# A two-block transformer kernel on one core: the first row's scale and shift moved to ScalarE, the start reordered, memory stores moved

## The chip, the cores and the metric

The kernel runs on one core of a Trainium2 chip (trn2). The metric is device time in microseconds (us), from one launch to its end; the number compared is the median of several runs. TensorE (PE), VectorE (DVE), ScalarE (ACT), GpSimd (POOL) and SyncE (SP) are the core's five engines. They run their own instruction streams in order and meet at semaphores. SP and POOL issue the DMAs here.

## What is computed

Two transformer blocks on 256 tokens of 1024 features, in float32. The first block is conditioned by a vector c: six slices of `silu(c) @ ada_w + ada_b` give a shift, a scale and a gate for each half of the block.

```python
mod = silu(c) @ ada_w + ada_b
shift1, scale1, gate1, shift2, scale2, gate2 = split(mod, 6)
u = rms_norm(h, norm1_g) * (1 + scale1) + shift1
z = u @ w_in                      # q, k, v of two attentions, gates
mixed = (sigmoid(m_a) * y_a + sigmoid(m_b) * y_b) @ w_out
h = h + gate1 * mixed
h = h + gate2 * (relu(rms_norm(h, norm2_g) * (1 + scale2) + shift2) @ w1)**2 @ w2
# second block: x + swiglu/2, then spatial gating + latent attention
# + attention over a memory of 256 rows (rms_norm(mem) @ w_kv), then x + swiglu/2
x = x + merged @ w_out_2
x = x + 0.5 * swiglu(rms_norm(x, ffn2_norm), w_gu, w_down)
```

## The kernel before

**Layout and stream.** Activations are kept feature-major: 8 blocks `k` of 128 features by 256 tokens. The weights arrive as one stream of slots of 8 tiles (128x1024 float32, 512 KB) in a ring of six. To keep float32 accuracy every operand is split in a rounded high part and a low part: ACT rounds a slot (L1413, `round_slot`), DVE subtracts (L1873, `split_slot`), and TensorE does three products per tile (hi·hi, hi·lo, lo·hi; `project`), or two with a 512 wide one (`project_wide`, hi times both parts side by side). Of the activations `u` and `u_lo` are the two parts. On ACT and DVE the call `ahead(name, reach)` puts the splitting of all slots up to the one that `name` uses, plus a reach, at this place of the engine's stream; `output`, `taken` do the same and wait for a PSUM bank to be full or freed.

**The first stage.** c (one row) goes through Tanh on ACT (L1488) and a multiply on DVE (L1948), TensorE spreads it over the partitions (`spread_c`), DVE copies it to `c_row` (L1953). Meanwhile ACT squares x, TensorE sums the squares (`x_ss`) and ACT makes `row_rinv` (L1454, L1456). Each of the 16 first columns of `mod` is one reduction of a 512 KB tile with `c_row` on DVE (`ada_sum`, L1929, an instruction and a short read of its accumulator): for each block k first the scale column, then the shift column. TensorE then runs one stage per block k, 48 matmuls of two slots (2k and 2k+1), once block k of `u` and `u_lo` is there. On DVE stage k reads: split of slot 2k, low part of u (L1975), split of slot 2k+1, the two `ada_sum` of block k+1, the scale column times the gain (L1967), and x times scale times `row_rinv` (L1969). On ACT: round slot 2k, add the shift and round (L1498), round slot 2k+1. TensorE fills the time at the start with matmuls on ones (`keep_warm`, 8 ahead of `spread_c`, 6 behind the small product `bias`, which needs the two small tables `buckets` and `table`).

**Further places.** POOL's stream holds the other 32 tiles of `ada` in a ring of three (L1316), the load of `bias` (L1334), the two stores of the memory's normalised parts (L1338, L1340), and their loads back. The stick-breaking attention works in `sbw`, 12 blocks of `wide`, at blocks 16 to 27, and starts once both memory stores have landed. In the last product of the second block's mix, `add_and_split` (L2182 adds the product to x, L2261 makes the low part of u) hands over to `project_first_two`, which takes two banks at once (f2g0, f2u0): the second is the bank of mix2_6. The last product `f2d7` is a `project_wide`, so two additions follow it (L2253, L2254) before the last store.

## Time and profile before

| | us |
|---|---|
| median of 3 runs | 1038.56 (1038.42 to 1039.31) |
| the profiled run | 1034.66 |
| its span, first to last instruction | 1032.9 |

The profile is of one run; its span lies 1.8 us under that run's own time, and that run lies 3.9 us under the median. Columns of a timeline row: start in us, length in us, engine, line, operation, output<-input, shape, how many in a row; in brackets the idle time of the engine before it and what ended it. A busy TensorE row is a modelled length; the distance between starts tells the pace.

### The profile page before, as it was taken

The numbers are of one execution on the slowest core, as the hardware profiler recorded it, in microseconds if no ns is written. First come the engines' busy times: TensorE is split into PE (matmuls) and PEld (weight loads), VectorE is DVE, ScalarE is ACT, GpSimd is POOL, SyncE is SP. The second block draws the span as 40 slices with busy tenths as digits, with TensorE's granted clock in tenths as the row PEclk, the third lists the DMA queues.
The fourth block names the chain that finished last, engine by engine and source line by source line (L and its number), as shares of the span: only waits on it lengthen the run. The fifth ranks groups of instructions, "written<-read, shape, count | busy, mean of one in ns | idle before, by whom it ended". The sixth has DMA issues, their size and how long they took to land.

```text
span 1032.9 us, 18991 instructions
## 1 busy us (share of the span) xinstructions
PE 1025.3 (99%) x6926; PEld 933.1 (90%) x6926; DVE 808.3 (78%) x1486; ACT 614.8 (60%) x1140; POOL 47.3 (5%) x74
## 2 busy tenths in 40 slices
PE   8999999999999999999999999999999999999998
PEld 7999998999988888888888899899999998888887
DVE  7998988988988555598887867666877869888753
ACT  5497688547665444565654557796554466555532
POOL 1011100020100000000000100000000010000000
PEclk9999999999999999999999999999999999999999
DMA  9998855776866666666666655555445546666663
GB/s 355 411 359 286 275 174 165 234 260 218 307 186 186 191 191 185 183 187 190 191 187 187 190 175 164 154 153 164 123 123 153 174 149 200 189 192 189 185 191 113
DMA packets 58366, 208.94 MB, mean 202 GB/s; under 512 B 7041, under 2 KB 8449, under 8 KB 57771
## 3 DMA queue, kind: packets, MB, share of 16 engines
q1 hardware_dynamic: 52474, 184.72, 58.2%
q0 software_dynamic: 5808, 23.09, 6.4%
q8 instruction: 55, 0.90, 0.4%
q14 instruction: 29, 0.23, 0.1%
HBM read 204.62 MB, written 3.16 MB: 201 GB/s over the span
## 4 chain that ended last, share of the span: by engine, by line
PE 92%; DVE 6%; issue 2%; ACT 1%; DVEq 0%; ACTq 0%
PE bank L682 90%; DVE ring_rounded L1873 2%; PE bank L1043 1%; DVE ada_ring L1929 1%; DVE body L1929 0%; DVE u L1969 0%; DVE u_rounded L1975 0%; ACT body L1573 0%; DVE body L1989 0%; ACT rounded_rounded L1413 0%; DVE body L2163 0%; ACT body L1505 0%; DVE body L2167 0%; DVE part L2163 0%; DVE body L2118 0%
## 5 line engine op out<-in xcount | busy, mean ns | idle before, releaser
L682 PE MATMUL bank<-u_rounded,rounded_rounded 128*128 128x256 f32 (+1 forms) x2152 | 506.8, 328 | 1.4 <-issue 1.0
L1873 DVE TENSOR_TENSOR ring_rounded<-ring,rounded_rounded 128x1024 fp32r<-128x1024 f32 x326 | 397.2, 1224 | 114.1 <-ACT rounded_rounded L1413 103.2
L1413 ACT ACTIVATE rounded_rounded<-ring 128x1024 fp32r<-128x1024 f32 x326 | 342.8, 1054 | 111.5 <-PE bank L682 100.6
L682 PE MATMUL bank<-u_rounded,ring_rounded 128*128 128x256 f32 x1504 | 350.3, 281 | 0.0
L682 PEld LDWEIGHTS bank<-u_rounded,rounded_rounded 128*128 128x128 f32 x2152 | 332.7, 188 | 4.9 <-issue 2.0
L682 PE MATMUL bank<-body_rounded,rounded_rounded 128*128 128x256 f32 (+1 forms) x1296 | 321.1, 335 | 0.2 <-DVE body L2163 0.2
L682 PEld LDWEIGHTS bank<-u_rounded,ring_rounded 128*128 128x128 f32 x1504 | 282.8, 188 | 37.1
L682 PE MATMUL bank<-body_rounded,ring_rounded 128*128 128x256 f32 x952 | 217.0, 280 | 0.0
L682 PEld LDWEIGHTS bank<-body_rounded,ring_rounded 128*128 128x128 f32 x952 | 178.9, 188 | 26.4
L682 PEld LDWEIGHTS bank<-body_rounded,rounded_rounded 128*128 128x128 f32 x1296 | 201.1, 188 | 1.4 <-issue 0.4
L1668 ACT ACTIVATE part<-bank 128x256 f32<-128x256 f32 x65 | 24.9, 383 | 78.5 <-PE bank L682 78.5
L1929 DVE CUSTOM_DVE_ANT_0 ada_ring<-ada_ring,ada_acc,cols 128x1024 f32<-128x1024 f32 x38 | 48.4, 1279 | 0.2 <-DMA ada_ring<-in_ada 0.2
L1361 POOL TENSOR_TENSOR turned<-turned 128x256 f32<-128x256 f32 x20 | 18.3, 914 | 572.3 <-ACT turned L1844 248.1
L2229 DVE TENSOR_TENSOR part<-bank,part 128x256 f32<-128x256 f32 x65 | 27.5, 424 | 17.5 <-ACT part L1668 17.4
L1573 ACT ACTIVATE body<-body,stats 128x128 f32<-128x128 f32 (+2 forms) x64 | 25.9, 407 | 15.4 <-DVE stats L2442 15.4
L1668 ACT ACTIVATE body<-bank 128x256 f32<-128x256 f32 x42 | 16.1, 383 | 31.8 <-PE bank L682 31.8
L1643 ACT ACTIVATE body_rounded<-body 128x256 fp32r<-128x256 f32 x76 | 31.2, 411 | 5.2 <-DVE body L2331 4.1
L2154 DVE TENSOR_TENSOR body_rounded<-body,body_rounded 128x256 fp32r<-128x256 f32 x76 | 31.8, 418 | 1.1 <-ACT body_rounded L1643 1.0
L682 PE MATMUL bank<-rounded_rounded,u_rounded 128*128 128x512 f32 (+1 forms) x96 | 28.1, 364 | 1.5 <-ACT lines L1502 1.5
L2229 DVE TENSOR_TENSOR body<-bank,body 128x256 f32<-128x256 f32 x42 | 17.8, 424 | 14.2 <-ACT body L1668 14.0
L1316 POOL DMA_DIRECT2D ada_ring<-in_ada x32 | 17.2, 537 | 173.7 <-DVE mod L1929 168.8
L682 PEld LDWEIGHTS bank<-rounded_rounded,u_rounded 128*128 128x128 f32 x96 | 17.0, 188 | 4.3 <-issue 1.7
(276 smaller groups left out, 892.2 us busy)
## 6 DMA issues: line engine op xcount, KB each, us to landing
ring<-in_stream SPq DMA_DIRECT2D x328, 512.0 KB, 3.7
ada_ring<-in_ada POOLq DMA_DIRECT2D x32, 512.0 KB, 5.4
body<-in_ada SPq DMA_DIRECT2D x8, 512.0 KB, 9.2
ada_ring<-in_ada SPq DMA_DIRECT2D x6, 512.0 KB, 8.3
mem_parts_kept<-body_rounded POOLq DMA_DIRECT2D x2, 1024.0 KB, 7.3
body_rounded<-mem_parts_kept POOLq DMA_DIRECT2D x2, 1024.0 KB, 5.2
x<-in_x_t SPq DMA_DIRECT2D x2, 512.0 KB, 4.7
body<-in_mem_t SPq DMA_DIRECT2D x2, 512.0 KB, 7.0
```

Of the source, the lines that this page charges most:

```text
L682: return nc.tensor.matmul(out, lhs, rhs, start=start, stop=stop, skip_group_check=True)
L1043: return nc.tensor.transpose(ps[:, at_col:at_col + P], src, mat("ident"))
L1316: pool.dma_start(ada_ring[:, n % ADA_RING, :], ada[ADA_EARLY + n]).then_inc(ada_full[n % ADA_RING], 16)
L1361: ins = pool.tensor_tensor(row_squares[:, i, :], row_squares[:, i - 1, :], row_squares[:, i, :], ALU.add)
L1413: a(R(slot_round(q)), slot_weights(n), ACT.Copy).then_inc(slot_rounded, 1)
L1573: ins = a(dst, src, ACT.Exp, scale=-1.0 if i < 8 else 1.0, bias=stats[:, i % 2, 0, k:k + 1], accum_out=stats[:, i % 2, 1, k:k + 1])
L1643: a(R(hidden[:, i, :]), hidden_lo[:, i, :], ACT.Copy).then_inc(hidden_rounded, 1)
L1668: a(dst, bank(name)[:, T:2 * T], ACT.Copy).then_inc(half_copied, 1)
L1873: v.tensor_tensor(R(w), w, R(slot_round(q)), ALU.subtract).then_inc(slot_split, 1)
L1929: v.tensor_tensor_reduce(out=w, in0=w, in1=c_row, scale=0.5, scalar=col("ada_b", at), op0=ALU.mult, op1=ALU.add, accum_out=mod[:, at:at + ...
L2154: v.tensor_tensor(R(hidden_lo[:, i, :]), hidden_lo[:, i, :], R(hidden[:, i, :]), ALU.subtract).then_inc(hidden_ready, 1)
L2229: free(v.tensor_tensor(dst, bank(name)[:, 0:T], dst, ALU.add), name)
```

## The change

- **c in two halves.** Tanh, multiply and copy of c are done for columns 0 to 511 and 512 to 1023 apart; the copies to `c_row` stand ahead of the wait for `cols`.
- **Slots 0 and 1 ahead of the small tables** in SP's order of loads.
- **Scale and shift on ACT.** DVE only multiplies x by `row_rinv` (`normed_x`), between the scale sum and the shift sum of a block. ACT makes scale times gain plus gain (128x1), then u rounded and u plain with scale and shift in one pass each (two 128x256), then rounds slot 2k+1. DVE's low part is a plain subtraction.
- **Two slots (16, 17) are split before DVE adds the memory's squares.**
- **Memory stores later and in parts**; `bias` is loaded after the first head of the stick-breaking attention is evacuated; `sbw` lies in blocks 12 to 23; `mats` is loaded in two parts, the second and `pos` by POOL.
- **In the second mix** both last additions to x come before low parts 4 to 6.
- **f2d7 is a plain `project`**, followed by one addition.

```diff
-MATRICES = ["ones", "ident", "halves", "q_even", "q_odd", "rotate", "neg_suffix",
-            "neg_ones", "before", "not_before", "not_after", "spread"]
+MATRICES = ["ones", "ident", "halves", "neg_suffix", "neg_ones", "before", "not_before", "spread",
+            "q_even", "q_odd", "rotate", "not_after"]
+LATE_MATRICES = 8
...
-        sbw = flat(wide[:, 16:28, :]).rearrange("p (a b c) -> p a b c", a=2, b=4)
+        sbw = flat(wide[:, 12:24, :]).rearrange("p (a b c) -> p a b c", a=2, b=4)
...
             for k in range(RING // 2):
                 load_ada_early(k)
+                for r in (2 * k, 2 * k + 1):
+                    load(r, r)
                 if k == 0:
                     sp.dma_start(buckets, buckets_d).then_inc(loaded["bias_in"], 16)
                     sp.dma_start(table[:, :], table_d).then_inc(loaded["bias_in"], 16)
-                for r in (2 * k, 2 * k + 1):
-                    load(r, r)
...
             load_ada(0, ADA_RING)
+            load_ada(ADA_RING, ADA_RING + ADA_IN_KEYS)
+            pool.wait_ge(u_rounded, ROW_MEM * KD + KD // 2)
+            pool.dma_start(mem_parts_kept[0, :, 0:4, :], R(mem_n[:, 0:4, :])).then_inc(mem_hi_stored, 16)
+            evacuated(pool, "cmp_hid_k")
+            load_ada(ADA_RING + ADA_IN_KEYS, ADA_RING + ADA_BEFORE_SB)
+            evacuated(pool, "sbz0")
+            pool.wait_ge(u_rounded, (ROW_MEM + 1) * KD)
+            pool.dma_start(mem_parts_kept[0, :, 4:8, :], R(mem_n[:, 4:8, :])).then_inc(mem_hi_end_stored, 16)
             pool.wait_ge(bias_stored, 16)
             pool.dma_start(bias, bass.AP(bias_rows.tensor, bias_rows.offset, [[1, P], [512, 8], [1, T]])
                            ).then_inc(loaded["bias"], 16)
-            load_ada(ADA_RING, ADA_RING + ADA_IN_KEYS)
-            pool.wait_ge(u_rounded, (ROW_MEM + 1) * KD)
-            pool.dma_start(mem_parts_kept[0], R(mem_n)).then_inc(mem_stored, 16)
+            load_ada(ADA_RING + ADA_BEFORE_SB, ADA_RING + ADA_BEFORE_SB + 2)
             pool.wait_ge(u_ready, (ROW_MEM + 1) * KD)
-            pool.dma_start(mem_parts_kept[1], R(mem_n_lo)).then_inc(mem_stored, 16)
+            pool.dma_start(mem_parts_kept[1], R(mem_n_lo)).then_inc(mem_lo_stored, 16)
...
-            a(c_tanh, c_line, ACT.Tanh, scale=0.5).then_inc(c_tanh_ready, 1)
+            for h in c_halves:
+                a(c_tanh[:, h], c_line[:, h], ACT.Tanh, scale=0.5).then_inc(c_tanh_ready, 1)
...
             for k in range(KD):
+                scale, shift, gain = mod[:, KD + k:KD + k + 1], mod[:, k:k + 1], col("norm1_g", k)
+                act.wait_ge(ada_summed, 2 * k + 1)
+                a(scale, scale, ACT.Identity, scale=gain, bias=gain).then_inc(scale_ready, 1)
                 ahead(f"u{k}", 1)
-                act.wait_ge(u_normed, ROW_X * KD + k + 1)
+                act.wait_ge(scale_ready, k + 1)
+                act.wait_ge(x_normed, k + 1)
                 act.wait_ge(ada_summed, 2 * k + 2)
-                a(R(u[:, k, :]), u_lo[:, k, :], ACT.Identity, bias=mod[:, k:k + 1]).then_inc(u_rounded, 1)
+                a(R(u[:, k, :]), u_lo[:, k, :], ACT.Identity, scale=scale, bias=shift).then_inc(u_rounded, 1)
+                a(u_lo[:, k, :], u_lo[:, k, :], ACT.Identity, scale=scale, bias=shift).then_inc(u_normed, 1)
                 ahead(f"u{k}", 2)
...
-            sum_early(0)
-            scaled(0)
+            def sum_early_with_x(k):
+                sum_early(2 * k)
+                if k == 0:
+                    dve.wait_ge(row_rinv_ready, ROW_X + 1)
+                normed_x(k)
+                sum_early(2 * k + 1)
+
+            sum_early_with_x(0)
             for k in range(KD):
                 ahead(f"u{k}", 1)
                 low_part_of_u(k)
                 ahead(f"u{k}", 2)
                 if k < KD - 1:
-                    sum_early(k + 1)
-                    scaled(k + 1)
+                    sum_early_with_x(k + 1)
+            ahead("vsw0", 3)
...
                 add_mixed(5)
                 ahead(f"{last}6")
+                add_mixed(6)
                 low_part(4)
+                add_mixed(7)
+                evacuated(dve, f"{last}{KD - 1}")
                 low_part(5)
-                add_mixed(6)
                 low_part(6)
                 ahead(f"{last}7")
-                add_mixed(7)
-                evacuated(dve, f"{last}{KD - 1}")
                 low_part(KD - 1)
...
-                    add_both(f"{p}d{m}", m, 0.5)
+                    if row == ROW_4 and m == KD - 1:
+                        add_residual(f"{p}d{m}", m, 0.5, reach=False)
+                    else:
+                        add_both(f"{p}d{m}", m, 0.5)
```

How the instructions stand on DVE at the first block and into the second, before (ISA on a 128x1024 tile is `ada_sum`, ISA on 128x1 its accumulator read; `ring_rounded` is the split of a slot):

```order
L1929 ISA ada_ring,mod<-ada_ring,ada_acc,cols 128x1024 [waits ada_early_full1]
L1929 ISA mod 128x1
L1967 SCALAR_TENSOR_TENSOR mod<-mod,cols 128x1 [waits ada_summed]
L1969 SCALAR_TENSOR_TENSOR u<-x,mod,row_rinv 128x256 [waits row_rinv_ready,dve_step]
L1873 TENSOR_TENSOR ring_rounded<-ring,rounded_rounded 128x1024 [waits slot_rounded]
L1975 SCALAR_TENSOR_TENSOR u_rounded<-u,mod,u_rounded 128x256 [waits u_rounded]
L1873 TENSOR_TENSOR ring_rounded<-ring,rounded_rounded 128x1024 [waits slot_rounded]
```

And in the change:

```order
L1950 ISA ada_ring,mod<-ada_ring,ada_acc,cols 128x1024 [waits ada_early_full0]
L1950 ISA mod 128x1
L1986 TENSOR_TENSOR u<-x,row_rinv 128x256 [waits row_rinv_ready]
L1950 ISA ada_ring,mod<-ada_ring,ada_acc,cols 128x1024 [waits ada_early_full1]
L1950 ISA mod 128x1
L1894 TENSOR_TENSOR ring_rounded<-ring,rounded_rounded 128x1024 [waits slot_rounded]
L1992 TENSOR_TENSOR u_rounded<-u,u_rounded 128x256 [waits u_normed,u_rounded]
```

The multiply of x, which waits for `row_rinv`, stood behind both sums of the block and now stands between them.

On ACT, the same stretch before, from the end of `row_rinv` on:

```order
L1456 ACTIVATE row_rinv<-log_ms 128x256 [waits bank_free0]
L1413 ACTIVATE rounded_rounded<-ring 128x1024 [waits slot_full0,row_rinv_ready]
L1498 ACTIVATE u_rounded<-u,mod 128x256 [waits ada_summed,u_normed]
L1413 ACTIVATE rounded_rounded<-ring 128x1024 [waits slot_full1]
L1502 ACTIVATE lines<-bank 8x512 [waits bank_full1]
```

And in the change:

```order
L1470 ACTIVATE row_rinv<-log_ms 128x256 [waits bank_free0]
L1512 ACTIVATE mod<-mod,cols 128x1 [waits ada_summed,row_rinv_ready]
L1427 ACTIVATE rounded_rounded<-ring 128x1024 [waits slot_full0]
L1517 ACTIVATE u_rounded<-u,mod 128x256 [waits ada_summed,x_normed,scale_ready]
L1518 ACTIVATE u<-u,mod 128x256
L1427 ACTIVATE rounded_rounded<-ring 128x1024 [waits slot_full1]
```

Two more instructions stand on ACT for each block, one of them between the rounding of u and that of slot 2k+1.

On DVE in the second mix, from the fifth addition on, before (bank 2 is mix2_6, bank 0 mix2_7):

```order
L2182 SCALAR_TENSOR_TENSOR x<-bank,x 128x256 [waits bank_full6]
L1873 TENSOR_TENSOR ring_rounded<-ring,rounded_rounded 128x1024 [waits slot_rounded]
L2261 SCALAR_TENSOR_TENSOR u_rounded<-x,cols,u_rounded 128x256 [waits u_rounded] x2
L2182 SCALAR_TENSOR_TENSOR x<-bank,x 128x256 [waits bank_full2]
L2261 SCALAR_TENSOR_TENSOR u_rounded<-x,cols,u_rounded 128x256 [waits u_rounded]
```

And in the change:

```order
L2204 SCALAR_TENSOR_TENSOR x<-bank,x 128x256 [waits bank_full6]
L1894 TENSOR_TENSOR ring_rounded<-ring,rounded_rounded 128x1024 [waits slot_rounded]
L2204 SCALAR_TENSOR_TENSOR x<-bank,x 128x256 [waits bank_full2]
L2283 SCALAR_TENSOR_TENSOR u_rounded<-x,cols,u_rounded 128x256 [waits u_rounded]
L2204 SCALAR_TENSOR_TENSOR x<-bank,x 128x256 [waits bank_full0]
L2283 SCALAR_TENSOR_TENSOR u_rounded<-x,cols,u_rounded 128x256 [waits u_rounded,bank_free0]
```

The addition that empties bank 2 moved ahead of two low parts.

## Rows read from the trace of the kernel before

**Rows 1.** Page, part 1: busy time and share of the span by engine.
```profile
PE 1025.3 (99%) x6926; PEld 933.1 (90%) x6926; DVE 808.3 (78%) x1486; ACT 614.8 (60%) x1140; POOL 47.3 (5%) x74
```

**Rows 2.** Timeline of TensorE (PEld its weight loads), from the start on.
```profile
1.14 3.61 PE L682 MATMUL bank<-mats 128*128 128x128 f32 x16 [1.14 <-DVE mats L1946]
...
10.24 0.09 PEld L682 LDWEIGHTS bank<-lines,table 33*8 33x8 f32 x2 [0.33 <-DMA table<-in_table]
...
11.19 1.60 PE L682 MATMUL bank<-mats 128*128 128x128 f32 x12
...
14.34 0.36 PE L682 MATMUL bank<-rounded_rounded,u_rounded 128*128 128x256 f32 x1 [1.55 <-ACT lines L1502]
```

**Rows 3.** Busy time in six stages: engines in us, PEclk, DMA share, GB/s.
```profile
20.20:54.40 34.20, 34.20 (x253) 32.52 (x252) 33.98 (x55) 15.18 (x19) 1.94 (x4) 1.00 1.02 409
```

**Rows 4.** Timeline of DVE, block 0.
```profile
11.46 0.48 DVE L1969 SCALAR_TENSOR_TENSOR u<-x,mod,row_rinv 128x256 f32<-128x256 f32 x1
...
13.60 0.48 DVE L1975 SCALAR_TENSOR_TENSOR u_rounded<-u,mod,u_rounded 128x256 fp32r<-128x256 f32 x1
```

**Rows 5.** Timeline of DVE, from block 1's last sum to block 2's second.
```profile
17.54 0.08 DVE L1929 DVE_READ_ACCUMULATOR2_ANT mod<- 128x1 f32 x1
...
17.73 0.48 DVE L1969 SCALAR_TENSOR_TENSOR u<-x,mod,row_rinv 128x256 f32<-128x256 f32 x1
...
19.26 0.48 DVE L1975 SCALAR_TENSOR_TENSOR u_rounded<-u,mod,u_rounded 128x256 fp32r<-128x256 f32 x1
19.74 1.23 DVE L1873 TENSOR_TENSOR ring_rounded<-ring,rounded_rounded 128x1024 fp32r<-128x1024 f32 x1
20.88 1.28 DVE L1929 CUSTOM_DVE_ANT_0 body<-body,ada_acc,cols 128x1024 f32<-128x1024 f32 x1
...
22.09 1.28 DVE L1929 CUSTOM_DVE_ANT_0 body<-body,ada_acc,cols 128x1024 f32<-128x1024 f32 x1
```

**Rows 6.** Timeline of ACT, end of row_rinv and block 1.
```profile
10.92 0.42 ACT L1456 ACTIVATE row_rinv<-log_ms 128x256 f32<-128x256 f32 x1
...
18.25 0.51 ACT L1498 ACTIVATE u_rounded<-u,mod 128x256 fp32r<-128x256 f32 x1 [0.87 <-DVE u L1969]
18.66 1.04 ACT L1413 ACTIVATE rounded_rounded<-ring 128x1024 fp32r<-128x1024 f32 x1
```

**Rows 7.** Timeline of TensorE, start of stage 7 and of the next product.
```profile
54.42 0.36 PE L682 MATMUL bank<-rounded_rounded,u_rounded 128*128 128x256 f32 x1
...
60.55 0.36 PE L682 MATMUL bank<-u_rounded,rounded_rounded 128*128 128x256 f32 x1 [0.23 <-DVE ring_rounded L1873]
```

**Rows 8.** Timelines of DVE, then TensorE, at the end of the second mix.
```profile
841.72 1.83 DVE L2261 SCALAR_TENSOR_TENSOR u_rounded<-x,cols,u_rounded 128x256 fp32r<-128x256 f32 x2
843.48 0.41 DVE L2182 SCALAR_TENSOR_TENSOR x<-bank,x 128x256 f32<-128x256 f32 x1
...
842.75 0.28 PE L682 MATMUL bank<-body_rounded,ring_rounded 128*128 128x256 f32 x1
843.99 0.36 PE L682 MATMUL bank<-u_rounded,rounded_rounded 128*128 128x256 f32 x1 [0.96 <-issue]
...
847.26 0.28 PE L682 MATMUL bank<-u_rounded,ring_rounded 128*128 128x256 f32 x1
847.57 0.39 PE L682 MATMUL bank<-u_rounded,rounded_rounded 128*128 128x256 f32 x1
```

**Rows 9.** Timeline of DVE at the end of the kernel.
```profile
1029.76 0.42 DVE L2253 SCALAR_TENSOR_TENSOR x<-bank,x 128x256 f32<-128x256 f32 x1 [6.78 <-PE bank L682]
1030.22 0.42 DVE L2254 SCALAR_TENSOR_TENSOR x<-bank,x 128x256 f32<-128x256 f32 x1
```

**Rows 10.** Timelines of DVE, then TensorE, in the stick-breaking attention (heads 3 to 5).
```profile
113.31 1.28 DVE L1929 CUSTOM_DVE_ANT_0 ada_ring<-ada_ring,ada_acc,cols 128x1024 f32<-128x1024 f32 x1 [0.15 <-DMA ada_ring<-in_ada]
...
115.32 0.28 DVE L2034 TENSOR_TENSOR body<-body,mats 128x128 f32<-128x128 f32 x1
...
118.18 1.14 PE L682 MATMUL bank<-body,mats 128*128 128x256 f32 x6
```

73 lines of the change are left out of this document (39 added, 34 removed).

## The prediction

> **What bounds the kernel now.** I read the busy shares first: TensorE 99% of the span [rows 1], nothing else above 90%. The chain of waits agrees: it runs through TensorE from 60.55 on but for a few knots. So only four kinds of time can move: the start until TensorE has its first real matmul (14.34 [rows 2]), the first eight stages if another engine paces them, the few holes later, and what stands behind the last matmul. Everything else, the memory stores among it, has TensorE's work as cover.
>
> In the first stages DVE is busy 33.98 of 34.20 us [rows 3] and repeats every 5.75 us (worked out below). TensorE's stage 0 begins at 14.34, stage 7 at 54.42 [rows 2, 7]: 40.08 for seven, 5.73 each. The six stages of [rows 3] have it busy for 34.20 us without a gap, so it needs 5.70 for one at most. The two are nearly level, and a slower loop on DVE or ACT shows at once.
>
> **Start-up.** Halving c gains almost nothing: the warm-up matmuls hold TensorE until 4.75 [rows 2], where c's product started anyway. I take 0.1 us, so `row_rinv`, done at 11.34 [rows 6], is done at 11.25. Then the order on DVE costs: the second sum now stands behind the multiply that waits for `row_rinv`, where before both sums were done by the time the multiply began (11.46 [rows 4]). The multiply has no row of its own kind; the nearest is the old one, 0.48 long [rows 5], of which some 0.08 overlaps the next; with one factor fewer I take 0.38 (bounds 0.34 and 0.40). Second sum 11.68 to 12.96 (1.28 [rows 5]); call its end t. ACT then makes its two passes and rounds slot 1, DVE splits slot 0 (1.14) and takes the low part (0.42): ready at 14.5 against 14.08. So the first stage could start 0.4 later.
>
> The small tables are a second brake. TensorE began `bias` at 10.24, after 0.33 of waiting for them [rows 2]. Behind slots 0 and 1, 1.05 MB, at 409 GB/s [rows 3] they come 2.6 us later, at 12.8. Bias to first warm-up is 0.95 (10.24 to 11.19), the warm-up 1.60 [rows 2]: stage 0 starts at about 15.3 instead of 14.34. That is 0.9 late, but TensorE can catch up as long as DVE is behind it.
>
> The granted clock is part of this. The 16 warm-up records at 1.14 take 3.61, the 12 at 11.19 take 1.60 [rows 2]: the first are at the 1.2 GHz level, the later at 2.4 GHz, and the 1.55 us of idleness before 14.34 did not lower it. Now the idleness lies ahead of `bias` and is 2.6 us long. The Trainium skill (TensorE: Matmul & The Clock Gate, What's actually happening) says that an idle array falls back to half rate. By that rule bias and warm-up may run at the lower level; the trace, with its shorter hole, doesn't decide it.
>
> **The loop of the eight stages.** Before, from t (17.62 in block 1): scale and multiply, ACT's shift at 18.25, its rounding of slot 2k+1 at 18.66 for 1.04, DVE's split at 19.74, sums at 20.88 and 22.09, the end 1.28 later at 23.37 [rows 5, 6]: 5.75. DVE's split waits for ACT here (19.74 is 0.04 after ACT's end). Now ACT's first pass can begin at t+0.04, the second 0.41 later, the rounding another 0.41 later (18.25 to 18.66), its end at t+1.90, the split at t+1.94 instead of t+2.12. But the multiply, 0.38, now stands between the sums: 1.94 + 1.14 + 1.21 + 0.38 + 1.28 = **5.95**. DVE has less work (it now idles about 0.35 per block behind ACT), yet the loop through both engines is 0.2 longer. The pass that was saved on DVE came back on ACT ahead of the rounding that DVE waits for.
>
> From there: block 1's t is 18.9 (12.96 + 5.95), block 7's 54.6, its low part 1.56 later (1.14 + 0.42) at 56.2, TensorE at most 0.26 behind that (14.34 after 14.08 in block 0); I take 56.3. Its last stage is 5.73 long like the others. End at 62.0. Before, the next product began at 60.55 instead of 60.15 (54.42 + 5.73), since DVE added the memory's squares before it split slot 16 [rows 7]. The change splits slots 16 and 17 first: ACT has slot 15 rounded at 56.5, then eight squares of at most 0.41 each, slot 16 by 60.8 at the latest, DVE splits it by 62.0, just in time. Sum of the first part: 62.0 - 60.55 = **+1.5 us**. The late start (15.3) is swallowed: 15.3 + 2 x 5.70 = 26.7, where DVE allows stage 2 at 26.5 and falls behind from then on.
>
> The Trainium skill (ScalarE: Activation LUTs, Rules for kernel authors) says to put additions and multiplications on VectorE. It speaks against this edit; the trace agrees only in part, since a pass is 0.51 on ACT and 0.48 on DVE [rows 5, 6]: the engine isn't dearer, the place is.
>
> **The second mix.** TensorE ends mix2_7 at 842.75 and starts f2g0 at 843.99, since the pair of banks needs mix2_6 added to x; that addition (843.48 to 843.89) stood behind two low parts of 0.92 each [rows 8]. Now it starts at 841.72 and the banks are free at 842.2, before TensorE arrives. A second, small wait follows: 847.26 to 847.57, for u's last block [rows 8]; its addition moves from behind a split to 843.1, so that goes too. Without both the 28 matmuls between run from about 842.95 and end at 846.35 instead of 847.57 (pace (847.26 - 843.99)/27 = 0.121, with the first a little longer): **-1.2 us**. Next are the low parts of blocks 5 to 7 on DVE, wanted from 846.8 on, ready by 846.6: bound 0 to 0.5 for that, I take 0.
>
> **The end.** One addition fewer: 1030.22 - 1029.76 = 0.46 [rows 9]. The plain product has 66 matmuls of 256 columns for 22 of 512 and 22 of 256: the same columns, 22 starts more. A start costs about 0.01 beyond its columns (0.118 pace against 0.107 for 256 columns at 2.4 GHz), 0.2 in all, less 0.1 for a shorter last one. **-0.3 us** (bounds -0.5 and -0.2).
>
> **Stores, `bias`, matrices, `sbw`.** POOL's queue gets other neighbours. `bias` is loaded some 40 us later, yet 20 us before its first use; ACT and DVE no longer wait for both stores at the first head, a wait that TensorE never felt. Zero, with the cover named in the second rival.
>
> **Sum.** +1.5 - 1.2 - 0.3 = 0.0. The span stays 1032.9, the profiled run 1034.7, and the median, to which I carry the difference, at 1038.5.
>
> **Rivals.**
> 1. *The first stages are not slower.* If ACT's second pass and rounding overlap more, or the multiply hides, TensorE paces: start 15.3, eight times 5.70, end 60.9, +0.4. Against it: ACT starts its instructions 0.41 apart in every row. Sum -1.1: 1037.4. It decides if the loop is under 5.7.
> 2. *The moved store collides, and the kernel is slower.* The 1 MB store of the low parts goes out near 105 us between tiles of `ada`. DVE waited for such a tile at 113.31 already (0.15), softplus of head 5 was done at 115.60, TensorE wanted it at 118.18 [rows 10]: cover 2.6 us. The store alone takes 2.6 us at 409 GB/s and 5 if it gets half. It decides from 2.6 us of delay; at 5 us TensorE loses 2.4. Sum +2.4: 1040.9.
> 3. *The clock drops in the hole before `bias`.* Bias and warm-up at the lower level are 0.95 + 1.6 longer, stage 0 at 17.8, eight stages of 5.70 to 63.4: 1.4 more than forecast, 1039.9. It decides if 2.6 us of idleness are enough where 1.55 were not. [...]
> 4. *The mix doesn't gain.* Should low part 4 (0.92, slowed) or the slot's split be late, half of 1.2 is left: 1039.1.
>
> **How the numbers follow.** Forecast 0.50, its own range 1037.8 to 1039.3 (the multiply 0.34 to 0.40 is 0.3 over seven blocks, the end 0.3, the low parts 0.5). Rival 1: 0.18. Rival 2: 0.14, the upper half of its price in doubt. Rival 3: 0.10. Rival 4: 0.08. A measurement of this kernel tells about 0.2%, 2.1 us, from no change. Only rival 2 at its full price, or two of the upper ones together, is slower by that: 0.13. Faster by that needs rival 1 with gains that I don't see: 0.07. Same: 0.80. The range reaches past rival 1 and most of rival 2: 1036.9 to 1040.7.
>
> **What the profile will show.** DVE's low part of u every 5.95 us with a gap of 0.3 to 0.4 put down to ACT's rounding before each split of an odd slot (right), or no gap and 5.70 (rival 1). `bias` on TensorE at 12.8, stage 0 at about 15.3, the next product at 62.0 with no hole. Warm-up records of 12 in 1.6 us or in 2.6 (rival 3). f2g0 less than 0.3 after mix2_7, and the end of the kernel 0.3 closer to the last matmul. Gaps of DVE before `ada_sum` near 115 would be rival 2. I am wrong if the first stages are paced by TensorE, or if a new hole over 0.5 us stands anywhere between 62 us and the mix.

## The result

The changed kernel is slower: 1043.13 us in the median of 15 runs (1038.68 to 1044.4), against 1038.98 (1034.8 to 1043.84) for the kernel before in 15 runs beside it. The ratio is 1.0035, with a 95% interval of 1.0019 to 1.0050. The profiled run took 1038.79 us with a span of 1037.1; before it was 1034.66 with 1032.9, so the trace shows 4.2 us to explain. The forecast was 1038.5, no change, with a range up to 1040.7. Both the time and the direction were wrong.

One thing must be known to read the times below. The runs of nearly every kernel here lie in two clusters some 4 us apart (before: 1034.7 to 1037.3 and 1038.2 to 1044.5; after: medians of 1038.79 and 1043.41), because TensorE's clock rises either by 5 us from the start of the span or only at 12.7 to 13.9; the section on the hardware shows it. So I compare the medians of the clusters, and traces from the end of this start on. All ratios are over all runs, and this spread makes their intervals wide.

| start of, us | before | after | difference |
|---|---|---|---|
| `row_rinv` on ACT | 10.92 | 11.03 | 0.1 |
| stage 0 on TensorE | 14.34 | 15.84 | 1.5 |
| the product behind the eight stages | 60.55 | 64.01 | 3.5 |
| the matmul on the sum of the memory's squares | 66.33 | 70.39 | 4.1 |
| attention, the product at 133.85 before | 133.85 | 139.37 | 5.5 |
| the part behind the attention, the product at 199.78 before | 199.78 | 205.66 | 5.9 |
| f2g0 behind the second mix | 843.99 | 848.82 | 4.8 |
| f2g0, last block of u | 847.57 | 852.14 | 4.6 |
| last addition to x | 1030.22 | 1034.36 | 4.1 |

Read downwards, the difference grows in three places (stages, squares, attention), a little in a fourth (0.4 by 200), and falls at the mix and at the end.

### The profile page after: what moved, and what is told of

The parts are those of the page before. It is cut to its first block, busy times and chain, and to the rows that moved or that the text cites. A ratio compares the mean times of both kernels' runs of the same rounds, so it can differ in the third digit from the quotient of the medians.

```text
span 1037.1 us, 19048 instructions
## 1 busy us (share of the span) xinstructions
PE 1027.4 (99%) x6948; PEld 935.5 (90%) x6948; DVE 805.5 (78%) x1478; ACT 621.5 (60%) x1157; POOL 49.4 (5%) x77
## 4 chain that ended last, share of the span: by engine, by line
PE 88%; DVE 7%; ACT 2%; issue 1%; DMA 1%; ACTq 0%; DVEq 0%
PE bank L685 87%; DVE ring_rounded L1894 2%; DVE ada_ring L1950 2%; PE bank L1046 1%; DVE body L1950 1%; ACT rounded_rounded L1427 1%; DMA ada_ring<-in_ada 1%; ACT u L1518 0%; ACT body L1593 0%; DVE u L1986 0%; DVE body L2053 0%; ACT body L1525 0%; DVE body L2011 0%; DVE body L2185 0%; DVE part L2185 0%
## 5 line engine op out<-in xcount | busy, mean ns | idle before, releaser
L685 PEld LDWEIGHTS bank<-body_rounded,rounded_rounded 128*128 128x128 f32 x1318 | 204.5, 188 | 1.7 <-DVE body L2185 0.7
```

The lines of the kernel that those rows point to most:

```text
L685: return nc.tensor.matmul(out, lhs, rhs, start=start, stop=stop, skip_group_check=True)
```

## The profile after

**The start and the first stages.** TensorE's timeline, answering to [rows 2]:

```profile
12.77 1.02 PE L685 MATMUL bank<-lines,table 33*8 33x512 f32 x2 [2.35 <-DMA table<-in_table]
13.72 1.87 PE L685 MATMUL bank<-mats 128*128 128x128 f32 x12
15.84 0.55 PE L685 MATMUL bank<-rounded_rounded,u_rounded 128*128 128x256 f32 x1 [0.24 <-issue]
...
22.74 0.28 PE L685 MATMUL bank<-rounded_rounded,u_rounded 128*128 128x256 f32 x1
```

The tables land at 12.8 as forecast. The 12 warm-up matmuls take 1.87 instead of 1.60 and the first matmul of stage 0 0.55 instead of 0.36: the clock went to its lower level behind the 2.35 us hole (granted clock 0.68 from 14.3 to 16 us, 0.71 from 16 to 20). Stage 0 lasts 6.90 (15.84 to 22.74) instead of some 5.8. Stage 0 begins 0.10 behind the end of ACT's copy of the small product (15.74); before, it waited for the same copy (14.25, start at 14.34 [rows 2]):

```profile
15.17 0.57 ACT L1522 ACTIVATE lines<-bank 8x512 f32<-8x512 f32 x1
```

DVE and ACT in block 1, answering to [rows 5] and [rows 6]:

```profile
19.18 1.22 DVE L1894 TENSOR_TENSOR ring_rounded<-ring,rounded_rounded 128x1024 fp32r<-128x1024 f32 x1
20.58 0.43 DVE L1992 TENSOR_TENSOR u_rounded<-u,u_rounded 128x256 fp32r<-128x256 f32 x1 [0.18 <-ACT u L1518]
21.46 1.23 DVE L1894 TENSOR_TENSOR ring_rounded<-ring,rounded_rounded 128x1024 fp32r<-128x1024 f32 x1 [0.45 <-ACT rounded_rounded L1427]
22.60 1.28 DVE L1950 CUSTOM_DVE_ANT_0 body<-body,ada_acc,cols 128x1024 f32<-128x1024 f32 x1
...
23.81 0.42 DVE L1986 TENSOR_TENSOR u<-x,row_rinv 128x256 f32<-128x256 f32 x1
24.14 1.28 DVE L1950 CUSTOM_DVE_ANT_0 body<-body,ada_acc,cols 128x1024 f32<-128x1024 f32 x1
```

```profile
19.38 0.60 ACT L1517 ACTIVATE u_rounded<-u,mod 128x256 fp32r<-128x256 f32 x1 [0.28 <-DVE mod L1950]
19.89 0.59 ACT L1518 ACTIVATE u<-u,mod 128x256 f32<-128x256 f32 x1
20.39 1.04 ACT L1427 ACTIVATE rounded_rounded<-ring 128x1024 fp32r<-128x1024 f32 x1
```

A pass with both operands takes 0.60, and the next starts 0.50 to 0.51 later, where [rows 6] have 0.51 and 0.41. DVE now waits twice in a block, 0.18 for the second pass and 0.45 for the rounding of the odd slot. The low part of block 0 began at 14.42, so a block takes 6.16. TensorE follows DVE from stage 5 on, as its wait before stage 7 shows:

```profile
58.15 0.36 PE L685 MATMUL bank<-rounded_rounded,u_rounded 128*128 128x256 f32 x1 [0.26 <-DVE u_rounded L1992]
...
67.47 0.47 PE L685 MATMUL bank<-u_rounded,rounded_rounded 128*128 128x256 f32 x2 [0.36 <-DVE ring_rounded L1894]
...
70.39 0.38 PE L685 MATMUL bank<-body,mats 128*128 128x256 f32 x1
```

The hole before 67.47 is new. On DVE the sums of the squares now stand where the next slot's split is wanted:

```profile
63.00 2.40 DVE L2011 TENSOR_TENSOR body<-body 128x1024 f32<-128x1024 f32 x3
...
66.11 1.22 DVE L1894 TENSOR_TENSOR ring_rounded<-ring,rounded_rounded 128x1024 fp32r<-128x1024 f32 x1
```

**The attention**, answering to [rows 10]. DVE's waits for tiles of `ada` (sum, number, longest), before and then after:

```profile
DVE ada_ring L1929 <- DMA ada_ring<-in_ada: 0.2, 1, 0.2
```

```profile
DVE ada_ring L1950 <- DMA ada_ring<-in_ada: 4.0, 2, 3.4
```

DMA issues from 104 to 124 (how many, KB, median us to landing), before and then after:

```profile
ada_ring<-in_ada POOLq DMA_DIRECT2D x8, 512.0 KB, 5.5
```

```profile
ada_ring<-in_ada POOLq DMA_DIRECT2D x6, 512.0 KB, 6.8
mem_parts_kept<-body_rounded POOLq DMA_DIRECT2D x1, 1024.0 KB, 9.6
```

The store went out at 108.67, the tile behind it at 112.00, and DVE could read that tile at 120.61. In TensorE's timeline this wait comes back as three holes, which put it 0.7, 0.4 and 0.35 us further behind the kernel before:

```profile
122.96 0.81 PE L685 MATMUL bank<-body,mats 128*128 128x256 f32 x3 [0.65 <-DVE body L2056]
...
128.22 0.70 PE L685 MATMUL bank<-body,mats 128*128 128x256 f32 x2 [0.31 <-DVE body L2056]
...
139.37 0.61 PE L1046 MATMUL bank<-mats,body 128*15 128x128 f32 x4 [0.53 <-DVE body L2140]
```

**The mix and the end**, answering to [rows 8] and [rows 9]. TensorE, then DVE:

```profile
848.70 0.28 PE L685 MATMUL bank<-body_rounded,ring_rounded 128*128 128x256 f32 x1
848.82 0.28 PE L685 MATMUL bank<-u_rounded,rounded_rounded 128*128 128x256 f32 x1
```

```profile
1034.36 0.42 DVE L2204 SCALAR_TENSOR_TENSOR x<-bank,x 128x256 f32<-128x256 f32 x1 [6.95 <-PE bank L685]
```

f2g0 starts 0.12 behind the last matmul of the mix, with no wait, and one addition closes the kernel.

## The experiments

My theory from this trace was a sum: the loop of the stages, which runs through ACT (+3.5 with the start), the squares ahead of a split (+0.5), the store between tiles (+1.5), the mix (-1.5), the end (-0.3). Its rivals were that the late start with its low clock costs the first part, and that the holes in the attention come from something else than the store.

Since the start differs from run to run, I measure the first part from the start of `row_rinv` to the start of the matmul on the squares' sum (10.92 and 66.33 before, 11.03 and 70.39 after):

| kernel | `row_rinv` | squares | first part | against before |
|---|---|---|---|---|
| before | 10.92 | 66.33 | 55.41 | |
| after | 11.03 | 70.39 | 59.36 | +3.95 |
| e1, old order on POOL | 10.71 | 70.07 | 59.36 | +3.95 |
| e2, scale on DVE | 11.15 | 66.59 | 55.44 | 0.0 |
| e3, roundings ahead | 11.11 | 73.42 | 62.31 | +6.9 |
| e4, mix and end alone | 14.89 | 70.30 | 55.41 | 0.0 |
| e5, tables first | 15.30 | 74.66 | 59.36 | +3.95 |
| e6, e3 mended | 15.41 | 73.36 | 57.95 | +2.5 |
| e7, no scale operand | 15.03 | 72.92 | 57.89 | +2.5 |
| e9, combined | 15.12 | 72.01 | 56.89 | +1.5 |
| e10, slots 16, 17 ahead | 15.10 | 70.14 | 55.04 | -0.4 |
| e12, POOL's order alone | 10.95 | 66.37 | 55.42 | 0.0 |
| e13, squares first | 15.09 | 74.58 | 59.49 | +4.1 |
| e14, as e4 | 15.51 | 70.93 | 55.42 | 0.0 |

Kernels without an edit in this part agree to 0.01 us, whatever the start (before, e4, e12, e14), so 0.1 us can be read here.

**e1, the old order on POOL's queue.**

```diff
             load_ada(0, ADA_RING)
-            load_ada(ADA_RING, ADA_RING + ADA_IN_KEYS)
-            pool.wait_ge(u_rounded, ROW_MEM * KD + KD // 2)
-            pool.dma_start(mem_parts_kept[0, :, 0:4, :], R(mem_n[:, 0:4, :])).then_inc(mem_hi_stored, 16)
-            evacuated(pool, "cmp_hid_k")
-            load_ada(ADA_RING + ADA_IN_KEYS, ADA_RING + ADA_BEFORE_SB)
-            evacuated(pool, "sbz0")
-            pool.wait_ge(u_rounded, (ROW_MEM + 1) * KD)
-            pool.dma_start(mem_parts_kept[0, :, 4:8, :], R(mem_n[:, 4:8, :])).then_inc(mem_hi_end_stored, 16)
             pool.wait_ge(bias_stored, 16)
...
-            load_ada(ADA_RING + ADA_BEFORE_SB, ADA_RING + ADA_BEFORE_SB + 2)
+            load_ada(ADA_RING, ADA_RING + ADA_IN_KEYS)
+            pool.wait_ge(u_rounded, (ROW_MEM + 1) * KD)
+            pool.dma_start(mem_parts_kept[0, :, 0:4, :], R(mem_n[:, 0:4, :])).then_inc(mem_hi_stored, 16)
+            pool.dma_start(mem_parts_kept[0, :, 4:8, :], R(mem_n[:, 4:8, :])).then_inc(mem_hi_end_stored, 16)
             pool.wait_ge(u_ready, (ROW_MEM + 1) * KD)
             pool.dma_start(mem_parts_kept[1], R(mem_n_lo)).then_inc(mem_lo_stored, 16)
...
-            load_ada(ADA_RING + ADA_BEFORE_SB + 2, ADA_NSA)
+            evacuated(pool, "cmp_hid_k")
+            load_ada(ADA_RING + ADA_IN_KEYS, ADA_NSA)
```

> The changed kernel with POOL's queue in the old order: bias loaded first, both memory stores right behind the keys' ada tiles, then all further ada tiles. Theory (the 1 MB store of the low parts, put between ada tiles, made one tile take 8.6 us and DVE waited 3.4 us for it): the holes of TensorE at 122.0 and 127.6 and the two at 138.6 and 204.9 go, 1.9 us less than the changed kernel, so span +2.3 against the kernel before. Rival (the stream of weights fills the DMA engines there whatever POOL issues, the share is 0.98): DVE waits for an ada tile as long as in the changed kernel, span +4.2, holes stay. Second rival (the stores collide in the old place too once the first stages are later): the holes move to 100 to 110, span +3 to +4.

Span 1035.7, 1.4 under the changed kernel; median 1041.47 us in 10 runs, ratio 1.0017 (0.9999 to 1.0036). Within the clusters it is 0.9 and 1.7 under the changed kernel (1037.84 and 1041.73 against 1038.79 and 1043.41). TensorE's difference from before stays at 3.7 us from 70 to 199: all three holes are gone. DVE's waits for tiles, and the tiles from 104 to 124:

```profile
DVE ada_ring L1946 <- DMA ada_ring<-in_ada: 1.2, 2, 1.0
```

```profile
ada_ring<-in_ada POOLq DMA_DIRECT2D x7, 512.0 KB, 5.1
```

The small hole near 200 stays (0.4), so of the 1.9 that I expected 1.5 came. POOL's new order is the cause of the 1.5. That within it the store is what counts is read from the traces (it stands right ahead of the tile that comes late); no run moves the store alone, and the 1 MB load of `bias`, issued at 100.52, moved with it.

This trace settles a second point. Its clock fell too (granted 0.50 from 14.3 to 16 us), and stage 0 began 5.07 us behind `row_rinv`, where the changed kernel has 4.81; yet its first part is 59.36 us, the same to the hundredth. While the loop paces, neither the start of stage 0 nor its clock shows.

**e12, the new order on POOL's queue alone**, on the kernel before: the edits of `sbw`, of the semaphores and of POOL's stream, of which these are a few lines.

```diff
-        sbw = flat(wide[:, 16:28, :]).rearrange("p (a b c) -> p a b c", a=2, b=4)
+        sbw = flat(wide[:, 12:24, :]).rearrange("p (a b c) -> p a b c", a=2, b=4)
...
+            load_ada(ADA_RING + ADA_BEFORE_SB, ADA_RING + ADA_BEFORE_SB + 2)
             pool.wait_ge(u_ready, (ROW_MEM + 1) * KD)
-            pool.dma_start(mem_parts_kept[1], R(mem_n_lo)).then_inc(mem_stored, 16)
+            pool.dma_start(mem_parts_kept[1], R(mem_n_lo)).then_inc(mem_lo_stored, 16)
```

> The kernel before with the new order on POOL's queue alone (stores in parts and later, bias behind them, the low parts' 1 MB store between ada tiles; with the place of sbw that this needs). Theory (that store delays an ada tile beyond the cover of 2.6 us): DVE waits 2 to 3.5 us for a tile near 117, TensorE gets holes of 0.4 to 1.1 us near 120 and 0.35 near 136, span +1.4 to +1.6. Rival (the holes came only because all of the attention was 4 us later in the changed kernel, against an unmoved stream): no holes, span 0.

Median 1039.87 us in 10 runs, ratio 1.0017 (0.9995 to 1.0038); in the clusters 1036.82 and 1040.92, where the kernel before had 1035.16 and 1039.31 beside it: +1.6 in both, as expected. The profiled run (1039.28, which I counted to the later cluster) has the early rise and shows more, one hole of 2.79 and the clock at the lower level around its end (granted 0.51 from 120.5 to 124, 6 matmuls in 2.07), +4.2 in all. Counted to the earlier cluster it makes the two differences 1.8 and 1.8. TensorE's timeline, DVE's waits for tiles, and the tiles from 104 to 124:

```profile
121.01 2.07 PE L683 MATMUL bank<-body,mats 128*128 128x256 f32 x6 [2.79 <-DVE body L2043]
```

```profile
DVE ada_ring L1938 <- DMA ada_ring<-in_ada: 5.6, 3, 4.8
```

```profile
ada_ring<-in_ada POOLq DMA_DIRECT2D x6, 512.0 KB, 8.5
```

POOL's order does this without any other edit, and its price varies with how long the tile takes: 3.4 us of waiting cost 1.5, 4.8 cost 2.8 and then another 1.4 of clock. The store took 12.2 us here.

**e2, scale and shift on DVE as before**, the rest as in the change.

```diff
-                a(scale, scale, ACT.Identity, scale=gain, bias=gain).then_inc(scale_ready, 1)
...
-                a(R(u[:, k, :]), u_lo[:, k, :], ACT.Identity, scale=scale, bias=shift).then_inc(u_rounded, 1)
-                a(u_lo[:, k, :], u_lo[:, k, :], ACT.Identity, scale=scale, bias=shift).then_inc(u_normed, 1)
+                a(R(u[:, k, :]), u_lo[:, k, :], ACT.Identity, bias=mod[:, k:k + 1]).then_inc(u_rounded, 1)
...
-            sum_early_with_x(0)
+            sum_early(0)
+            scaled(0)
```

> The changed kernel with scale and shift of the first row done as before (scale column and one multiply with two factors on DVE behind both sums, shift alone on ACT), all else changed. Theory (the loop through ACT's two passes of 0.60 each is what makes the block 6.16 us): the block is 5.75 again, but TensorE starts at 15.8 and at a low clock, so it paces; stage 7 at about 56.9, next product at 62.6 instead of 64.0: -1.4 us against the changed kernel. Rival (the late start and the clock alone cost the 3.5 us): stages as in the changed kernel, 64.0, no difference.

Span 1033.1, 4.0 under the changed kernel, far more than the 1.4 I expected; median 1037.33 us in 10 runs, ratio 0.9991 (0.9968 to 1.0014).

```profile
13.03 1.02 PE L685 MATMUL bank<-lines,table 33*8 33x512 f32 x2 [2.49 <-DMA table<-in_table]
13.99 1.60 PE L685 MATMUL bank<-mats 128*128 128x128 f32 x12
15.35 0.36 PE L685 MATMUL bank<-rounded_rounded,u_rounded 128*128 128x256 f32 x1
...
66.59 0.38 PE L685 MATMUL bank<-body,mats 128*128 128x256 f32 x1
```

The tables are as late as in the changed kernel and stage 0 starts 1.0 late, yet the whole first part is as long as before. I had taken the low clock of stage 0 for granted, and here it didn't come; from then on TensorE gains on the kernel before, 0.8 behind at stage 7 and 0.3 at the next product. So the 3.95 us of the first part, the hole at 67 included, hang on scale and shift being on ACT, with the order on DVE that goes with it. How much would be left with a low clock in stage 0 this trace doesn't show.

**e5, the tables ahead of slots 0 and 1 again.**

```diff
                 load_ada_early(k)
-                for r in (2 * k, 2 * k + 1):
-                    load(r, r)
                 if k == 0:
                     sp.dma_start(buckets, buckets_d).then_inc(loaded["bias_in"], 16)
                     sp.dma_start(table[:, :], table_d).then_inc(loaded["bias_in"], 16)
+                for r in (2 * k, 2 * k + 1):
+                    load(r, r)
```

> The changed kernel with the two small tables loaded ahead of slots 0 and 1 again, as before. Theory (the late tables and the low clock of stage 0 are swallowed, since DVE and ACT pace the stages from stage 5 on at 6.16 us): the small product at 10.3 instead of 12.8 and stage 0 at 15.0 or earlier at the full clock, but the next product still at 64.0, no gain, span +4.2 against the kernel before. Rival (the late start costs the 3.5 us): next product at 60.5 to 61.0, span about +1.

One run, 1044.57 us, span 1041.5, in the later cluster, where the changed kernel has 1043.0 to 1044.4. Its first part is 59.36 us long, to the hundredth the changed kernel's. The tables' place costs nothing. Stage 0, which I expected at 15.0 or earlier, began 4.81 us behind `row_rinv`, exactly as in the changed kernel, since it waits for ACT's copy of the small product (L1522), and that stands behind both passes and the rounding of slot 1. Nor did it spare the clock: TensorE idles ahead of stage 0 instead, and the clock falls there (granted 0.57 from 20 to 24 us):

```profile
20.11 0.38 PE L685 MATMUL bank<-rounded_rounded,u_rounded 128*128 128x256 f32 x1 [2.93 <-ACT lines L1522]
...
21.78 0.63 PE L685 MATMUL bank<-ring_rounded,u_rounded 128*128 128x512 f32 x1
```

**e7, the passes without their scale.** The scale of the first row isn't applied; the 128x1 instruction that makes it stays.

```diff
-                a(R(u[:, k, :]), u_lo[:, k, :], ACT.Identity, scale=scale, bias=shift).then_inc(u_rounded, 1)
-                a(u_lo[:, k, :], u_lo[:, k, :], ACT.Identity, scale=scale, bias=shift).then_inc(u_normed, 1)
+                a(R(u[:, k, :]), u_lo[:, k, :], ACT.Identity, bias=shift).then_inc(u_rounded, 1)
+                a(u_lo[:, k, :], u_lo[:, k, :], ACT.Identity, bias=shift).then_inc(u_normed, 1)
```

> The changed kernel with the scale operand left out of ACT's two passes over u (they only add the shift, so the scale of the first row isn't applied; the 128x1 scale instruction stays). Theory (an ACTIVATE with a scale and a bias pointer takes 0.60 us where one with a bias alone takes 0.51): both passes 0.51, the rounding of the odd slot 0.18 earlier, the block 5.98 instead of 6.16, seven blocks -1.3 us, next product at about 62.8. Rival (0.60 comes from the unrounded source or from the traffic on memory): 0.60 stays.

ACT and DVE, blocks 3 and 4:

```profile
35.16 0.51 ACT L1517 ACTIVATE u_rounded<-u,mod 128x256 fp32r<-128x256 f32 x1 [0.28 <-DVE mod L1950]
35.58 0.49 ACT L1518 ACTIVATE u<-u,mod 128x256 f32<-128x256 f32 x1
```

```profile
36.17 0.42 DVE L1992 TENSOR_TENSOR u_rounded<-u,u_rounded 128x256 fp32r<-128x256 f32 x1
...
42.15 0.43 DVE L1992 TENSOR_TENSOR u_rounded<-u,u_rounded 128x256 fp32r<-128x256 f32 x1
```

The passes are 0.51 and 0.49 and a block 5.98, as expected, and the first part is 1.5 shorter (1.3 expected). The scale operand costs 0.09 us on each pass, with the same source, output and traffic. The Trainium skill (ScalarE: Activation LUTs, What ACT_TABLE_LOAD costs) says that each per-partition pointer operand adds about 93 ns; the trace agrees, and I had not priced it.

**e3, ACT rounds the next block's slots ahead.**

```diff
                 a(u_lo[:, k, :], u_lo[:, k, :], ACT.Identity, scale=scale, bias=shift).then_inc(u_normed, 1)
-                ahead(f"u{k}", 2)
+                ahead(f"u{k}", 4)
```

> The changed kernel, but ACT rounds the two slots of the next block ahead of that block's scale, so that the rounding of an odd slot no longer stands behind the two passes with scale and shift. Theory (the order on ACT, not DVE's work, makes the block 6.16): a block takes 5.70, the pace of TensorE, DVE's gap of 0.45 ahead of the odd slot's split goes, next product at 62.6 instead of 64.0, and since slots 16 and 17 are rounded before the memory's squares the hole of 0.5 at 67 goes too: -1.9 us against the changed kernel. Rival (DVE's own instructions are the bound): 6.1 as before, no difference but the hole, -0.5.

It was slower than the changed kernel: span 1040.9, median 1044.43 us in 10 runs, ratio 1.0047 (1.0029 to 1.0064). ACT shows why:

```profile
16.70 1.06 ACT L1427 ACTIVATE rounded_rounded<-ring 128x1024 fp32r<-128x1024 f32 x1 [1.37 <-DMA ring<-in_stream]
17.93 1.06 ACT L1427 ACTIVATE rounded_rounded<-ring 128x1024 fp32r<-128x1024 f32 x1 [0.17 <-DMA ring<-in_stream]
18.89 0.57 ACT L1522 ACTIVATE lines<-bank 8x512 f32<-8x512 f32 x1
```

The copy of the small product (L1522) now stood behind two roundings that waited for their loads, and TensorE began stage 0 only at 19.56. The edit had moved a second thing past the queue: my mistake. It says little of the loop, since TensorE, this late, paced the stages itself (7.8 behind the kernel before at stage 1, 7.2 at the next product).

**e6, the same with that copy in its old place** (block 0 alone: copy first, then `ahead("u0", 4)`).

> As e3_round_ahead (ACT rounds the two slots of the next block ahead of that block's scale), but in block 0 the copy of the small product is put ahead of those roundings, since in e3 it stood behind two roundings that waited for their loads, and TensorE waited for it until 19.5. Theory: stage 0 at 15.8 as in the changed kernel, every stage 5.70 from there on (with 1.1 for the low clock), next product at 62.6 and no hole at 67, -1.9 us against the changed kernel, span about 1035.2. Rival (the roundings ahead make ACT wait for slots that TensorE hasn't used yet, and delay the scale of the next block): stages of 6 us or more, no gain.

Median 1040.03 us in 10 runs, ratio 1.0019 (0.9997 to 1.0041). In the clusters 1037.06 and 1042.57, so 1.7 and 0.8 under the changed kernel; its first part is 1.4 shorter, where 1.9 was expected. DVE, blocks 3 and 4:

```profile
36.21 0.42 DVE L1993 TENSOR_TENSOR u_rounded<-u,u_rounded 128x256 fp32r<-128x256 f32 x1 [0.17 <-ACT u L1518]
36.55 1.22 DVE L1895 TENSOR_TENSOR ring_rounded<-ring,rounded_rounded 128x1024 fp32r<-128x1024 f32 x1
...
41.82 0.42 DVE L1993 TENSOR_TENSOR u_rounded<-u,u_rounded 128x256 fp32r<-128x256 f32 x1 [0.17 <-ACT u L1518]
```

The odd slot's split follows the low part at once, and a block takes 5.61 (36.21 to 41.82): level with TensorE or under it. DVE's own work was never the bound; ACT's order was. What is left of the first part's excess, 2.5, is the late stage 0 (4.81 behind `row_rinv`, where before has 3.42: 1.4) and its low clock (another 1.5), less 0.4 that TensorE made good later.

**e13, the squares ahead of the splits as before.**

```diff
-            ahead("vsw0", 3)
             dve.wait_ge(row_squares_ready, (ROW_MEM + 1) * KD)
```

> The changed kernel without its moved splits: DVE adds the memory's squares ahead of the splits of slots 16 and 17, as before. Theory (the new order opens the 0.5 us hole at 67 and takes away one of 0.3 before the next product at 64.0): that product 0.3 to 0.4 later, the hole at 67 gone, span within 0.2 of the changed kernel. Rival (the hole at 67 comes from slot 18's late rounding on ACT, not from DVE's order): the hole at 67 stays and a second one comes on top, +0.4.

One run, 1044.1 us, span 1041.2. The first part is 59.49 instead of 59.36. The hole at 67 is gone and its length stands ahead of the product instead, which is 0.7 later (0.3 to 0.4 expected):

```profile
68.80 0.48 PE L685 MATMUL bank<-u_rounded,rounded_rounded 128*128 128x256 f32 x2 [0.69 <-DVE ring_rounded L1894]
```

The moved splits neither gain nor lose: with DVE this late, whatever comes second is missed.

**e4, mix and end alone**, on the kernel before (with the plain `project` for `f2d7` too).

```diff
                 ahead(f"{last}6")
+                add_mixed(6)
                 low_part(4)
+                add_mixed(7)
+                evacuated(dve, f"{last}{KD - 1}")
                 low_part(5)
-                add_mixed(6)
                 low_part(6)
                 ahead(f"{last}7")
-                add_mixed(7)
-                evacuated(dve, f"{last}{KD - 1}")
...
+                    if row == ROW_4 and m == KD - 1:
+                        add_residual(f"{p}d{m}", m, 0.5, reach=False)
```

> The kernel before with two parts of the change alone: the order of the additions in the second mix, and the plain last product with one addition. Theory (they gain what the traces of both kernels say, whatever stands ahead): span -1.5 for the mix and -0.2 to -0.3 for the end, -1.7 against the kernel before. Rival (the mix gained in the changed kernel only because its stream of weights had fallen behind or ahead): less than 0.8 in all.

Median 1033.51 us in 9 runs, ratio 0.9973 (0.9945 to 1.0001). Most of that median is luck with the start (5 of its 9 runs are in the earlier cluster, 10 of 30 beside it): in the clusters it has 1033.38 and 1038.77 against 1035.53 and 1039.74, -2.2 and -1.0. The trace is the better witness. It fell in the later cluster, stands 3.98 us behind the kernel before from 60 on, and then, from f2g0 (847.10) and its last block of u (850.41) on, 3.11 and 2.84 behind; with the drift of 0.2 on the way to the mix that is -1.1 and -0.3 (and -0.1 in the matmul after). Its span is 1035.4, so of 4.0 to 4.2 us 2.5 are left: **-1.5 to -1.7 for mix and end**, as expected, and the same as in the changed kernel.

> The kernel of e4 once more, for a narrower interval and a trace with an early rise of the clock. Expected: -1.5 to -1.7 us against the kernel before, ratio 0.9983 to 0.9986. Rival: the earlier median of -5.6 us was more than chance, ratio below 0.997.

Median 1037.72 us in 12 runs, ratio 0.9994 (0.9975 to 1.0014), clusters 1034.82 and 1039.15 against 1035.16 and 1039.31: -0.3 and -0.2. Its trace has the same gain at f2g0: 5.81 us behind before at the end of mix2_7, 4.70 at f2g0 and 4.47 at its last block. But from `row_rinv` to the end it is only 0.5 shorter than the trace of before, where e4's is 1.5 shorter: it lost 0.75 at 74 and some 0.4 between 700 and the mix, where nothing was edited. The gain at the mix is there in every trace with this order; the times can't confirm 1.5 us in so wide a spread, and this kernel is not shown faster by them.

**e10, the same with slots 16 and 17 rounded and split ahead of the squares.**

```diff
-                ahead(f"u{k}", 2)
+                ahead(f"u{k}", 2 if k < KD - 1 else 4)
...
+            ahead(f"u{KD - 1}", 4)
             dve.wait_ge(row_squares_ready, (ROW_MEM + 1) * KD)
```

> The kernel before with the mix order, the plain last product and, new, slots 16 and 17 rounded by ACT and split by DVE ahead of the memory's squares, since TensorE waits 0.4 us for slot 16 before its next product there and the squares are wanted only at 70. Theory: that product starts at 60.2 instead of 60.55 and nothing else moves: span -1.5 -0.3 -0.35, some -2.0 us against the kernel before. Rival (the squares come too late then, or a hole of 0.5 opens at 63 to 67 as in the changed kernel): -1.5, no better than the mix and the end alone.

Median 1036.92 us in 12 runs, ratio 0.9983 (0.9962 to 1.0004), clusters 1032.84 and 1038.83, so 2.3 and 0.5 under the kernel before beside it. Not shown faster either. The first part is 0.37 shorter, as expected, but 2 us later TensorE waits for slot 18:

```profile
72.30 0.48 PE L682 MATMUL bank<-u_rounded,rounded_rounded 128*128 128x256 f32 x2 [1.56 <-DVE ring_rounded L1874]
```

```profile
69.84 1.06 ACT L1414 ACTIVATE rounded_rounded<-ring 128x1024 fp32r<-128x1024 f32 x1 [2.21 <-DMA ring<-in_stream]
```

Slot 18 landed late in a stretch with a DMA share of 1.02 (64 to 72 us; before has 1.02 there too). In all, this trace is 0.9 longer from `row_rinv` on than that of before. e14's trace loses 0.75 in the same place (from the matmul on the squares' sum to that on the keys' squares it takes 4.03, 70.93 to 74.96, where before took 3.28, 66.33 to 69.61), so this isn't e10's alone, but whether the edit makes it likelier stays open.

**e9, combined:** tables first, old order on POOL, roundings ahead, in block 0 both sums ahead of the multiply and the copy of the small product ahead of the first pass.

> A version meant to beat both: the changed kernel with the tables ahead of slots 0 and 1, the old order on POOL's queue, both sums of block 0 ahead of the multiply that waits for row_rinv, the copy of the small product ahead of the first pass, and ACT rounding two slots ahead as in e6. Theory: stage 0 at 13.6 to 14.2 (before 14.34), every stage 5.70 at TensorE's pace, no hole before the next product, which starts at 59.3 to 59.9 (before 60.55); the mix and the end give -1.2 and -0.2: span 1030.3 to 1031.0, -2 to -2.6 us against the kernel before. Rival (the loads of slots and tiles, 2.1 MB for each stage, don't come faster than every 5.73 us): first part as before, span 1031.4, the same as with the mix and the end alone.

Median 1036.29 us in 12 runs, ratio 0.9998 (0.9981 to 1.0014). It doesn't beat the kernel before. Stage 0:

```profile
19.03 0.36 PE L685 MATMUL bank<-rounded_rounded,u_rounded 128*128 128x256 f32 x1 [2.04 <-DVE u_rounded L1988]
...
21.42 0.63 PE L685 MATMUL bank<-ring_rounded,u_rounded 128*128 128x512 f32 x1
```

Behind the hole of 2.04 the clock was low until 23.3 (granted 0.50 from 20 on), and TensorE lost 1.54 there (19.03 is 4.69 behind before, 23.48 is 6.23), as much as the excess of its first part, 1.5. By my estimate from these two numbers the first part would be level with before without it: with the loop mended the edit buys nothing, as TensorE is the bound either way.

## Why the prediction was wrong

**The loop, the term that failed.** I wrote 5.95 per block and +1.5 at the end of the stages. Measured: 6.16 and +3.5. The step is "the second 0.41 later, the rounding another 0.41 later": I took the pace of [rows 6], a pass with a bias alone, for a pass with bias and scale. Two passes at 0.50 make the loop 0.18 longer, and e7 gave back 0.18 per block, 1.5 us in all. Two smaller errors go opposite ways: the first pass starts 0.12 behind the end of the sum's read and not 0.04, and the multiply holds up the next sum for 0.34 instead of 0.38 (it took 0.42, over my upper bound of 0.40, but the next starts 0.34 after it). Together a block is 0.21 longer than forecast, 1.5 us in seven. The rest of the 2.0: block 0's sum ended at 13.11 instead of 12.96, the low part waits 0.18 for the second pass, and from stage 7 to the next product it took 5.86 instead of 5.73. The mechanism (the work came back on ACT ahead of the rounding that DVE waits for) was right, and e6 and e2 show it.

**The squares, given nothing.** I had slot 16 split "just in time" and gave nothing for what stands behind. The forecast product had no hole, measured 0.1; but the squares' sums then pushed the next split, +0.6. e13 shows that it would have been lost either way.

**Stores "zero", the second term that failed.** I named the right transfer, the right cover (2.6 us) and the right victim as the second rival, and gave it 0.14. The tile kept DVE waiting for 3.4 us, 0.8 more than the cover; TensorE lost 0.7 there and 0.4 and 0.35 in the two holes behind, 1.5 in all. The error lies in the transfer's time: I took 2.6 us for a store alone and 5 for one that gets half, where it took 9.6, and the tile behind it could be read 8.6 us after its issue. The DMA share from 104 to 124 was 0.89 already before, and 0.98 now.

**The start and the third rival.** Stage 0 was forecast at 15.3 and came at 15.84. I let it wait for the tables and for the two parts of u, and gave nothing for ACT's copy of the small product, though [rows 2] name it as what stage 0 waits for (L1502): with the passes ahead of it that copy ends at 15.74, which is later than the tables allow (15.35 in e2), so e5, with the tables early, gained nothing. The clock fell as the rival says (in e2 it didn't). All of this was swallowed, since the loop was slower still, as e1 and e5 show.

**Mix and end** were right: -1.2 forecast and -1.4 to -1.5 measured for the mix, here and in e4; -0.3 forecast and -0.3 measured for the end (the first addition after `f2d6` starts 4.43 behind, 1026.53 against 1022.10, and the last one of the kernel 4.14 behind). The low parts behind the mix cost nothing, so the fourth rival has nothing to show.

**The median.** I carried the difference of the spans to the median. That held, 4.2 us in the spans and 4.1 in the medians, but with luck: both kernels had most of their runs in the later cluster (12 of 15 before, 10 of 15 after). Within the clusters the difference is 3.9 and 4.2.

The sum as it should have been: +4.1 (start, loop, squares), +1.5 (store), +0.4 (near 200), +0.1 of drift, -1.5 (mix), -0.3 (end): +4.3, where the spans say +4.2. The cause of the 0.4 near 200 stays open. It is there, 0.3 to 0.4 us, in every trace with scale and shift on ACT (after, e1, e3, e5, e6, e7, e9, e13) and in none of the others, so it seems to belong to that edit too.

## What to carry to other kernels

Work moved off a busy engine isn't gone if the busy engine waits for the other one: write the chain of one iteration through both, and price each instruction by a row with the same operands. Before a large store is moved into a stretch where the DMA engines are as busy as here (0.89), look at which load stands behind it in its queue and how long its reader can wait. And before an engine's late start is counted as a loss, ask which engine paces: only then does the start, or its clock, show in the end.
